# A Griffin-style decoder layer with a 32-expert mixture: the last two experts interleaved, and the attention scores' first part moved ahead of a weight split

## The chip, the cores and the metric

One core of one Trainium2 chip. The metric is the device time of one execution in microseconds (us), the median of three runs.

## The reference, cut to what matters

Batch 1, 256 tokens, width 1024, everything in fp32. First comes a mixing part, then a mixture of 32 experts, of which each token uses four, then a final RMSNorm:

```python
h = rmsnorm(x, norm_mix); proj = h @ w_in            # 1024 x 10256
# three branches: mLSTM (4 heads), forgetting attention (8 heads), memory attention (4 heads)
merged = sum_b sigmoid(gate_b) * (y_b @ w_branch[b]);  x = x + merged @ w_out
logits = t @ w_router + b_router;  top_v, top_i = top_k(logits, 4)     # t = rmsnorm(x, norm_moe)
combine = one_hot(top_i) weighted by softmax(top_v)
for each expert:                                     # w1 1024 x 2048, w2 1024 x 1024
    u = t @ w1 + b1
    g = minimum(u[:, :1024], 7);  lin = clip(u[:, 1024:], -7, 7)
    a = g * sigmoid(1.702 * g) * (lin + 1)
    out += combine[:, e] * (a @ w2 + b2)
return rmsnorm(x + out, norm_final)
```

## The kernel before, in words

Each engine runs its own instruction list; the order on each is the written order, and semaphores join them. There is no planner.

**Mixing part (about 0 to 422 us).** The projections are cut into 64 slots (`SLOTS`), two to each 2 MB unit of weights in a ring of three. ACT rounds a slot's weights (`round_weights`, L689), DVE subtracts to get the remainder (`split_weights`, L1024: 128x2048, called for slot i + 2 in slot i), and PE runs the three products of the parts (`project`). A table `STAGES` hangs other work behind the slots: for head h, `ml_scores` in slot 12+h, `fx_scores` in 24+h, `ca_scores` in 36+h, then turn and values one and two slots later. In each slot DVE does `drain(i)`, `split_weights(i + 2)` and then the stage's functions. A score function on DVE has a first part that ACT waits for (mask and row maximum, or bias and clamp, L1152, L1154, L1241 to L1244, L1250, L1251), a wait for ACT's exponential (for ml also for POOL's mask, L613), and a last part that PE waits for (L1161, or L1235 and L1237).

**Experts (about 422 us to the end).** Each expert's weights come as six 2 MB pieces, four of w1 (`W1`) and two of w2 (`W2`), into ten places used in turn; two spare places take the first two pieces of expert 25. SP issues piece n into a place when the piece ten earlier in it has been used (`place_used`). Up to 64 tokens of an expert are gathered. A product is `both_halves` (L1753, L1754): two matmuls with 64 stationary columns each, side by side on the array, for the low and high half of the output; one fp32 matmul is two instructions. PE's list for one expert is: layer one (four pieces), `gather` of the next tokens but one (same lines, from `sel`), `put` of the previous result into the four sum banks (L1871), turning the activations (L1836), biases (L1782, L1776), layer two's first piece, `turn_gathered` (L1766), its second piece, `turn_weighted` (L1812). DVE does the activation (L1361 to L1373), ACT the copies out of PSUM (L933 to L958). Experts 0 to 24 are in a loop, 25 to 31 are written out; after expert 25's layer one `add_tokens` (L1876) adds the residual to the sums.

**End.** `is_last` marks expert 31: its last w1 piece and last w2 piece come in halves (L468, L469, L472, L473), and its activations are turned in two parts. Then ACT copies the result (L958), PE does the last `put`, ACT squares the four 512-column sums (L981, `accum_out`) and takes the square root (L985), DVE multiplies by the inverse root and `norm_final` straight out of PSUM (L1439), and four DMAs write the output (L568, L570 on SP, L988 on ACT). `norm_final`, spread over 128 partitions (`gfin`, 512 KB), is loaded behind all weights (L543).

```python
def is_last(m, q):
    return isinstance(m, int) and m * TURN + q == NE - 1
for i in range(len(SLOTS)):            # DVE
    if i < len(SLOTS) - 1:
        drain(i)
    split_weights(i + 2)
    for name, *arg in STAGES.get(i, []):
        if name in work:
            work[name](*arg)
```

Of the kernel before, what the change touches and what calls it, by code (L numbers as in the profile page):

```python
# [4 lines left out]
F32 = mybir.dt.float32  # L5
# [6 lines left out]
P = 128  # L12
# [23 lines left out]
SPARE_PIECE = LOOPED * TURN * PIECES  # L36
CYCLE = TURN * PIECES // RING_PLACES
# [107 lines left out]
def build(nc, x, mem, norm_mix, w_in, b_ml_gates, conv_ml, ml_head_norm, b_fx_gate, norm_mem,  # L145
# [3 lines left out]
    with ctx:  # L149
# [6 lines left out]
        bank = [ctx.enter_context(nc.psum_tensor(f"bank{b}", [P, 512], F32)) for b in range(8)]  # L156
# [117 lines left out]
        with nc.sbuf_tensor("sq_dump", [P, TT, 2, 512], F32) as sq_dump:  # L274
# [23 lines left out]
        gfin = place[1][:, 0, :]  # L298
        results, final_dump = place[2][:, 0:TT, :], place[3][:, 0:TT, :]
# [11 lines left out]
        router_in, b1_in, b2_in, final_in, final_late_in, out_sent = (  # L311
            sem(n) for n in ("router_in", "b1_in", "b2_in", "final_in", "final_late_in", "out_sent"))
# [11 lines left out]
        ml_ready = sem("ml_ready")  # L324
        pre_zero = sem("pre_zero")
        conv_sum, conv_sig, qk_ready = sem("conv_sum"), sem("conv_sig"), sem("qk_ready")
        gate_lin, gate_log, gates_ready = sem("gate_lin"), sem("gate_log"), sem("gates_ready")
        act_step = sem("act_step")
        col_ready = sem("col_ready")
        ml_arg, ml_exp, ml_masked = sem("ml_arg"), sem("ml_exp"), sem("ml_masked")  # L330
        ml_num, ml_ms, ml_std, ml_y = sem("ml_num"), sem("ml_ms"), sem("ml_std"), sem("ml_y")
        max_ready, exp_ready, prob_ready, pt_ready, y_ready = (sem(n) for n in ("max_ready", "exp_ready", "prob_ready", "pt_ready", "y_ready"))
# [18 lines left out]
        final_ready = sem("final_ready")  # L351
        late_in = {j: sem(f"late_in{j}") for j in (W1 - 1, PIECES - 1)}
        late_actT, late_aT = sem("late_actT"), sem("late_aT")
# [56 lines left out]
        def is_last(m, q):  # L410

            return isinstance(m, int) and m * TURN + q == NE - 1

        def for_experts(eng, r, expert):

            with eng.Fori(0, LOOPED) as m:
                for q in range(TURN):
                    expert(r, m, q)
            for q in range(NE - LOOPED * TURN):
                expert(r, LOOPED + q // TURN, q % TURN)  # L420

# [25 lines left out]
        def _(sp):  # L447
# [5 lines left out]
            def load(e, j, b):  # L453

                halves = isinstance(e, int) and e == NE - 1 and j in late_in
# [9 lines left out]
                if halves and j < W1:  # L465

                    dst, src = (a.rearrange("p (q h n) -> p q h n", q=2, h=2) for a in (dst, src))
                    sp.dma_start(dst[:, :, 0], src[:, :, 0]).then_inc(late_in[j], 16)  # L468
                    sp.dma_start(dst[:, :, 1], src[:, :, 1]).then_inc(place_in[b], 16)  # L469
                elif halves:  # L470

                    sp.dma_start(dst[:, 0:2 * D], src[:, 0:2 * D]).then_inc(late_in[j], 16)  # L472
                    sp.dma_start(dst[:, 2 * D:4 * D], src[:, 2 * D:4 * D]).then_inc(place_in[b], 16)  # L473
                else:
                    sp.dma_start(dst, src).then_inc(place_in[b], 16)
# [65 lines left out]
            def load_final(loaded):  # L541

                sp.dma_start(gfin, norm_final.partition_broadcast(P)).then_inc(loaded, 16)  # L543
# [4 lines left out]
            for c in range(RING_PLACES, NE * PIECES - (LOOPED - 1) * TURN * PIECES):  # L548
                if not is_spare(LOOPED - 1, c):
                    load_piece(0, LOOPED - 1, c)  # L550
            sp.wait_ge(route_ready, 1)
            busiest = sp.value_load(most[0:1, 0:1], min_val=0, max_val=S)
            with sp.If(busiest < CAP + 1):
                sp.wait_ge(place_used[1], place_uses(1))
                load_final(final_in)
            with sp.If(busiest > CAP):
                with sp.Fori(1, ROUNDS) as r:
                    with sp.If(busiest > r * CAP):
                        with sp.Fori(0, LOOPED) as m:
                            for c in range(TURN * PIECES):  # L560
                                load_piece(r, m, c)
                        for c in range(NE * PIECES - SPARE_PIECE):
                            load_piece(r, LOOPED, c)
                sp.wait_ge(moe_end, 1)
                load_final(final_late_in)
# [3 lines left out]
            sp.wait_ge(final_ready, 4)  # L569
# [82 lines left out]
        def _(act):  # L652
# [277 lines left out]
            def expert(r, m, q):  # L930
                n = r * NE + m * TURN + q
                act.wait_ge(gate_ready, n + 1)
                act.activation(acts.rearrange("c (q p) -> c q p", q=4), gate, ACT.Sigmoid, scale=ALPHA).then_inc(sig_ready, 1)  # L933

                def keep_chosen():

                    act.wait_ge(selT_done, n + 1)
                    src = bank[LINEAR if is_last(m, q) else TURNS]
                    act.activation(selWT, src[:, 0:S].rearrange("p (t n) -> p t n", t=TT), ACT.Copy).then_inc(selWT_ready, 1)

                if is_last(m, q):
                    act.wait_ge(late_actT, r + 1)
                    act.activation(aT[:, 0:2], bank[TURNS][:, 0:2 * P].rearrange("p (q h c) -> p q h c", q=2, h=2),
                                   ACT.Copy).then_inc(late_aT, 1)
                    if isinstance(r, int):
                        warm(ACT.Sqrt)
                    act.wait_ge(act_turned, n + 1)
                    act.activation(aT[:, 2:4], bank[GATE][:, 0:2 * P].rearrange("p (q h c) -> p q h c", q=2, h=2),
                                   ACT.Copy).then_inc(aT_ready, 1)
                    keep_chosen()  # L950
                else:
                    keep_gathered(n + 2)
                    act.wait_ge(act_turned, n + 1)
                    act.activation(aT, bank[TURNS][:, :].rearrange("p (q h c) -> p q h c", q=4, h=2),
                                   ACT.Copy).then_inc(aT_ready, 1)
# [3 lines left out]
                if not is_last(m, q):  # L959
                    keep_chosen()  # L960
# [4 lines left out]
            def experts(r):  # L965
                for_experts(act, r, expert)

                act.wait_ge(got_ready, (r + 1) * NE)
                act.sem_inc(round_end, 1)

            def finish(rounds):

                if rounds:
                    warm(ACT.Sqrt)
                for t in range(TT):
                    for j in range(2):
                        if rounds:
                            act.wait_ge(moe_end, 1)
                        else:
                            act.wait_ge(put_done, 4 * NE + 2 * t + j + 1)  # L980
                        act.activation(final_dump[:, t, UW * j:UW * (j + 1)], bank[SUMS + 2 * t + j][:, :], ACT.Square,  # L981
                                       accum_out=ss[:, t, j:j + 1]).then_inc(final_sq, 1)
                    act.wait_ge(final_sq, 2 * t + 2)
                    act.wait_ge(final_var, t + 1)
                    act.activation(std[:, t, 0:1], ss[:, t, 1:2], ACT.Sqrt, bias=var[:, t:t + 1],  # L985
                                   scale=1.0 / D).then_inc(final_std, 1)
                act.wait_ge(final_ready, 3)
# [5 lines left out]
        def _(dve):  # L993
# [153 lines left out]
            def ml_scores(h):  # L1147
                dve.wait_ge(filled[5], turn(5, ("ml_m", h)))
                if h == 0:
# [5 lines left out]
                                  ALU.add, ALU.min).then_inc(drained[5], 1)  # L1155
                dve.wait_ge(ml_masked, 2 * h + 2)
# [82 lines left out]
            def fx_scores(h):  # L1239
# [4 lines left out]
                dve.tensor_reduce(negmax[:, 1:2], p_a[:, 128:384], AX.X, ALU.max, negate=True).then_inc(max_ready, 1)  # L1244
                dve.wait_ge(exp_ready, 2 * h + 2)
                normalise(((0, 128), (128, 384)))

            def ca_scores(h):
                dve.wait_ge(filled[4], turn(4, ("ca_s", h)))
                step(dve.tensor_reduce(negmax[:, :], bank[4][:, :].rearrange("p (t m) -> p t m", t=TT), AX.X, ALU.max))  # L1250
                dve.tensor_scalar(negmax[:, :], negmax[:, :], -CA_SCALE, None, ALU.mult).then_inc(max_ready, 1)  # L1251
                dve.wait_ge(exp_ready, 2 * FX_H + h + 1)
# [7 lines left out]
            for i in range(len(SLOTS)):  # L1260
# [3 lines left out]
                split_weights(i + 2)  # L1264
                for name, *arg in STAGES.get(i, []):
                    if name in work:
                        work[name](*arg)
# [79 lines left out]
            def take_turned(k):  # L1347
# [3 lines left out]
                for h in range(2):  # L1351
                    dve.tensor_tensor(gotT[:, :, h, :],  # L1352
                                      bank[TURNS][:, :].rearrange("p (q h c) -> p q h c", q=4, h=2)[:, :, h, :],
# [3 lines left out]
            def expert(r, m, q):  # L1357
                e = m * TURN + q
                n = r * NE + e
# [7 lines left out]
                blocks = acts.rearrange("c (q p) -> c q p", q=4)  # L1367
                dve.tensor_tensor(blocks, blocks, gate, ALU.mult).then_inc(ffn_step, 1)
                b, used = piece_turn(r, m, PIECES * q + W1 - 1)
# [6 lines left out]
                if not is_last(m, q):  # L1376
                    dve.wait_ge(gather_done, n + 2)
                    select(e + 2)
                    take_turned(n + 2)
                dve.wait_ge(selT_done, n + 1)  # L1380
                select_weighted(e + 1)

# [30 lines left out]
            def experts(r):  # L1413
                for_experts(dve, r, expert)
                dve.wait_ge(sel_ready, (r + 1) * (2 * (NE + 1)))
                dve.wait_ge(selW_ready, (r + 1) * (2 * (NE + 1)))
# [9 lines left out]
            def finish(rounds):  # L1426
# [3 lines left out]
                dve.wait_ge(final_late_in if rounds else final_in, 16)  # L1430
                for t in range(TT):
                    dve.wait_ge(final_sq, 2 * t + 1)
                    dve.tensor_scalar(var[:, t:t + 1], ss[:, t, 0:1], 1.0 / D, EPS, ALU.mult, ALU.add).then_inc(final_var, 1)
# [3 lines left out]
                    for j in range(2):  # L1437
# [479 lines left out]
```

## Time and profile before

| | us |
|---|---|
| median of three runs (lowest, highest) | 1327.95 (1327.43, 1328.49) |
| the profiled execution's own time | 1328.85 |
| its span, first to last instruction | 1326.9 |
| PE busy (share of the span) | 1291.2 (97%) |
| mean granted PE clock | 0.998 |

The profile is one execution. Times in its rows count from the start of its span. PE is the matmul engine and PEld its weight loads; a row of the time line is start, duration, engine, line, operation, output<-input, and in brackets how long the engine sat idle before it and who released it. Matmuls overlap, so the distance between two starts, and not the duration, is what one costs in a row.

### The profile page before, as it was taken

The numbers are of one execution on the slowest core, as the hardware profiler recorded it, in microseconds if no ns is written. First come the engines' busy times: TensorE is split into PE (matmuls) and PEld (weight loads), VectorE is DVE, ScalarE is ACT, GpSimd is POOL, SyncE is SP. The second block draws the span as 40 slices with busy tenths as digits, with TensorE's granted clock in tenths as the row PEclk, the third lists the DMA queues.
The fourth block names the chain that finished last, engine by engine and source line by source line (L and its number), as shares of the span: only waits on it lengthen the run. The fifth ranks groups of instructions, "written<-read, shape, count | busy, mean of one in ns | idle before, by whom it ended". The sixth has DMA issues, their size and how long they took to land.

```text
span 1326.9 us, 15133 instructions
## 1 busy us (share of the span) xinstructions
PE 1291.2 (97%) x6183; PEld 659.7 (50%) x6183; DVE 412.7 (31%) x736; ACT 323.4 (24%) x499; POOL 29.4 (2%) x42
## 2 busy tenths in 40 slices
PE   8999999999999999999999999999999999999997
PEld 8888888888887333333333333333333333333332
DVE  6864665545565121111211121111121111112112
ACT  5665555654444010100101010100011001001012
POOL 4000000000102000000000000000000000000000
PEclk9999999999999999999999999999999999999999
DMA  9553453536679999999999999999999999999996
GB/s 325 193 188 132 186 177 141 204 115 259 206 294 432 428 431 429 432 432 430 432 431 432 431 431 432 431 431 431 433 431 431 431 431 432 429 432 431 430 430 266
DMA packets 68030, 475.12 MB, mean 358 GB/s; under 512 B 7504, under 2 KB 9616, under 8 KB 43408
## 3 DMA queue, kind: packets, MB, share of 16 engines
q1 hardware_dynamic: 65840, 473.28, 85.9%
q10 hardware_dynamic: 2144, 1.21, 0.3%
q8 instruction: 31, 0.51, 0.1%
q14 instruction: 15, 0.12, 0.0%
HBM read 473.42 MB, written 1.05 MB: 358 GB/s over the span
## 4 chain that ended last, share of the span: by engine, by line
PE 75%; DMA 22%; DVE 1%; ACT 1%; issue 1%; SPq 0%; POOL 0%; DVEq 0%; ACTq 0%; POOLq 0%
PE bank L1753 37%; DMA place<-in_w_exp_in 22%; PE bank L1562 18%; PE bank L1541 4%; PE bank L1871 4%; PE bank L1542 2%; PE bank L1549 1%; PE bank L1836 1%; PE bank L1766 1%; PE bank L1776 1%; PE bank L1754 1%; DMA ring<-in_w_in 1%; PE bank L1685 1%; PE bank L1704 1%; PE bank L1812 1%
## 5 line engine op out<-in xcount | busy, mean ns | idle before, releaser
L1753 PE MATMUL bank<-place,fxqT 128*64 128x512 f32 x1520 | 677.5, 596 | 20.5 <-DMA place<-in_w_exp_in 19.5
L1754 PE MATMUL bank<-place,fxqT 128*64 128x512 f32 x1520 | 677.8, 596 | 0.0
L1753 PEld LDWEIGHTS bank<-place,fxqT 128*64 128x64 f32 x1520 | 198.3, 137 | 429.1 <-issue 389.1
L1754 PEld LDWEIGHTS bank<-place,fxqT 128*64 128x64 f32 x1520 | 198.3, 137 | 0.0
L1024 DVE TENSOR_TENSOR w_lo<-ring,w_hi 128x2048 fp32r<-128x2048 f32 x63 | 145.2, 2305 | 103.1 <-ACT w_hi L689 102.9
L689 ACT ACTIVATE w_hi<-ring 128x2048 fp32r<-128x2048 f32 x63 | 120.8, 1917 | 117.0 <-PE bank L1562 105.2
L1361 DVE TENSOR_SCALAR bank<-bank 128x512 f32<-128x512 f32 x32 | 22.4, 700 | 391.6 <-PE bank L1754 391.6
L1562 PE MATMUL bank<-w_hi,h_cat 128*128 128x512 f32 x448 | 141.1, 391 | 0.0
L933 ACT ACTIVATE fxqT<-bank 128x512 f32<-128x512 f32 x32 | 19.1, 598 | 414.1 <-DVE bank L1361 414.1
L1562 PEld LDWEIGHTS bank<-w_hi,h_cat 128*128 128x128 f32 x448 | 84.1, 188 | 17.4
L1352 DVE TENSOR_TENSOR fxqT<-bank,g_rows 128x256 f32<-128x256 f32 x64 | 24.2, 420 | 216.0 <-PE bank L1766 216.0
L1562 PE MATMUL bank<-w_lo,h_cat 128*128 128x512 f32 x224 | 87.2, 389 | 0.0
L1562 PE MATMUL bank<-w_hi,o_cat 128*128 128x512 f32 x256 | 82.0, 395 | 0.0
L958 ACT ACTIVATE yS<-bank 128x512 f32<-128x512 f32 x32 | 19.1, 598 | 249.3 <-PE bank L1754 249.3
L1541 PE MATMUL bank<-h_cat,w_hi 128*128 128x512 f32 x192 | 69.0, 402 | 0.0
L1871 PE MATMUL bank<-yS,fxqT 64*128 64x512 f32 x264 | 65.6, 615 | 0.8 <-ACT yS L958 0.8
L1753 PE MATMUL bank<-xs,sel 128*64 128x512 f32 x128 | 60.2, 592 | 0.2 <-DVE sel L1328 0.2
L1754 PE MATMUL bank<-xs,sel 128*64 128x512 f32 x128 | 60.2, 593 | 0.0
L1542 PE MATMUL bank<-h_cat,w_lo 128*128 128x256 f32 x192 | 53.9, 281 | 0.0
L1562 PEld LDWEIGHTS bank<-w_hi,o_cat 128*128 128x128 f32 x256 | 48.1, 188 | 10.2 <-DVE w_lo L1024 0.3
L1339 DVE TENSOR_SCALAR cols_wr<-slots_f,rank,comb 128x128 f32<-128x128 f32 x66 | 19.9, 344 | 106.8 <-PE bank L1812 106.8
L1562 PE MATMUL bank<-w_lo,o_cat 128*128 128x512 f32 x128 | 49.8, 389 | 0.0
(291 smaller groups left out, 1065.5 us busy)
## 6 DMA issues: line engine op xcount, KB each, us to landing
place<-in_w_exp_in SPq DMA_DIRECT2D x125, 2048.0 KB, 36.7
place<-in_w_exp_out SPq DMA_DIRECT2D x63, 2048.0 KB, 37.6
ring<-in_w_in SPq DMA_DIRECT2D x19, 2048.0 KB, 7.5
ring<-in_w_branch SPq DMA_DIRECT2D x6, 2048.0 KB, 7.7
ring<-in_w_mem_kv SPq DMA_DIRECT2D x4, 2048.0 KB, 7.7
ring<-in_w_out SPq DMA_DIRECT2D x2, 2048.0 KB, 11.1
spare<-in_w_exp_in SPq DMA_DIRECT2D x2, 2048.0 KB, 12.2
ring<-in_w_in SPq DMA_DIRECT2D x2, 1024.0 KB, 8.2
```

The costliest lines, as they stand in the source:

```text
L689: act.activation(hi, whole, ACT.Copy).then_inc(weights_rounded, 1)
L933: act.activation(acts.rearrange("c (q p) -> c q p", q=4), gate, ACT.Sigmoid, scale=ALPHA).then_inc(sig_ready, 1)
L1024: dve.tensor_tensor(lo, whole, hi.bitcast(F32), ALU.subtract).then_inc(weights_split, 1)
L1339: ins = dve.tensor_scalar(selW[:, t, :, :], twice, rank[:, t, bass.ds(e, 1)], comb[:, t, bass.ds(e, 1)], ALU.is_equal, ALU.mult)
L1352: dve.tensor_tensor(gotT[:, :, h, :], bank[TURNS][:, :].rearrange("p (q h c) -> p q h c", q=4, h=2)[:, :, h, :], weights[:, :, h].unsqueez ...
L1361: dve.tensor_scalar(bank[GATE][:, :], bank[GATE][:, :], LIMIT, None, ALU.min).then_inc(gate_ready, 1)
L1541: mm(slot_bank(i, c)[:, :], wh[:, k, tile], both, start=(k == 0), stop=False)
L1542: ins = mm(slot_bank(i, c)[:, 0:S], wl[:, k, tile], hi[:, k, :], start=False, stop=(k == KT - 1))
L1562: ins = mm(slot_bank(i, c)[:, :], stationary, moving, start=(k == 0 and n == 0), stop=(k == KT - 1 and n == 2))
L1753: mm(o[0:CAP, :], lhsT, low, start=start, stop=stop)
L1754: return mm(o[CAP:P, :], lhsT, high, start=start, stop=stop)
L1871: mm(bank[SUMS + q][:, :], selWT[half, t, :], yS[half, :], start=False, stop=last).then_inc(put_done, 1)
```

## The change: what it does

Two edits. **One**: the DVE functions `ml_scores`, `fx_scores` and `ca_scores` now call `split_weights(i + 2)` themselves, between their first part and their wait for ACT; in slots without scores it stays where it was. **Two**: `expert` runs experts 0 to 29 only, and `last_two` runs 30 and 31. Their pieces come, and are used, in the order w1 of 30, w1 of 31, w2 of 30, w2 of 31. The last w2 is loaded and computed by output halves: columns 0:512 of both pieces (1 MB each), then columns 512:1024 of the first piece (1 MB) and of the second in two row parts (512 KB each). So these are products of 256 columns a side, summed in the banks LINEAR and GATE; each half is copied and put into the sums on its own (`put_late`), and the squares of the first half's sums, and its product with `norm_final`, are made before the second half. `norm_final` comes as one 4 KB row behind a piece of expert 27 and is spread on PE with a column of ones in experts 27 and 28, DVE keeping the result (`GFIN_AT`); PE waits for that copy each time. At the end the unscaled results lie in SBUF and are scaled there, three quarters on DVE and one on ACT.

```diff
+LAST_ORDER = [(NE - 2 + n // W1, n % W1) for n in range(2 * W1)] + [(NE - 2 + n // W2, W1 + n % W2) for n in range(2 * W2)]
+GFIN_AT = (LOOPED * TURN + 2, LOOPED * TURN + 3)
+HALF = 256
@@ SP
+            def load_last_two(r):
+                for e, j in LAST_ORDER[:-W2]:
+                    b, used = late_turn(r, e, j)
+                    sp.wait_ge(place_used[b], used)
+                    load(e, j, b)
...
+                for j in range(W2):
+                    load_chunk(j, 0, slice(0, 4), place_in[late_turn(r, NE - 1, W1 + j)[0]])
+                load_chunk(0, 1, slice(0, 4), late_in[0])
+                for n in range(2):
+                    load_chunk(1, 1, slice(2 * n, 2 * n + 2), late_in[1 + n])
@@ DVE
-            def fx_scores(h):
+            def fx_scores(h, i):
...
                 dve.tensor_reduce(negmax[:, 1:2], p_a[:, 128:384], AX.X, ALU.max, negate=True).then_inc(max_ready, 1)
+                split_weights(i + 2)
                 dve.wait_ge(exp_ready, 2 * h + 2)
...
+                if isinstance(e, int) and e in GFIN_AT:
+                    h = GFIN_AT.index(e)
+                    dve.wait_ge(gfin_turned, r * 2 + (h + 1))
+                    dve.tensor_copy(gfin[:, 512 * h:512 * (h + 1)], bank[RESULT][:, :]).then_inc(gfin_kept, 1)
...
+            def keep_scaled(t, h, kept):
+                cut = slice(512 * h, 512 * (h + 1))
+                dve.tensor_tensor(results[:, t, cut], sums[:, t, h, :], gfin[:, cut], ALU.mult).then_inc(kept, 1)
@@ DVE, finish
+                    dve.wait_ge(put_done, 4 * NE + 4)
+                    keep_scaled(1, 1, final_kept)
+                    dve.wait_ge(final_sq, 1)
+                    keep_scaled(0, 1, final_kept)
...
-                    for j in range(2):
-                        dve.scalar_tensor_tensor(out=results[:, t, cut], in0=bank[SUMS + 2 * t + j][:, :], ...
+                    for j in range(t, 2):
+                        dve.tensor_scalar(results[:, t, cut], results[:, t, cut], rstd[:, t, 0:1], None, ALU.mult).then_inc(final_ready, 1)
@@ ACT, finish
+                    act.activation(dump, src, ACT.Square, accum_out=ss[:, t, 1:2]).then_inc(final_sq, 1)   # t = 1 waits for final_kept
...
+                act.activation(results[:, 1, 0:UW], results[:, 1, 0:UW], ACT.Copy, scale=rstd[:, 1, 0:1]).then_inc(final_scaled, 1)
@@ PE, in expert, between turn_acts and add_late_bias
+                if isinstance(e, int) and e in GFIN_AT:
...
+                    mm(bank[RESULT][:, :], ones_row, gfin_row[:, 512 * h:512 * (h + 1)], start=True, stop=True).then_inc(gfin_turned, 1)
+                    pe.wait_ge(gfin_kept, r * 2 + (h + 1))
@@ PE
+            def last_two(r):
+                layer_one(n, lambda j: late_turn(r, e, j))
...
+                gather(n * 2 + 4); put(n); turn_gathered(n + 2, RESULT)
+                turn_acts(acts, TURNS); add_biases(r, n + 1); add_late_bias(r, n)
+                layer_one(n + 1, lambda j: late_turn(r, e + 1, j))
+                layer_two(0, *late_turn(r, e, W1))
+                turn_weighted(r, n); turn_acts(acts_late, GATE); add_half_bias(LINEAR, 0)
+                turn_weighted(r, n + 1); add_half_bias(GATE, 1)
+                layer_two(1, *late_turn(r, e, W1 + 1))
...
+                chunk(bank[LINEAR], b0, 0, range(4), 0, False)
+                put(n + 1)
+                chunk(bank[LINEAR], b1, 1, range(4), 0, True).then_inc(chunk_done, 1)
+                chunk(bank[GATE], b0, 0, range(4), 1, False).then_inc(place_used[b0], 1)
+                put_late(r, 0)
+                for h in range(2):
+                    pe.wait_ge(late_in[1 + h], r * 16 + 16)
+                    ins = chunk(bank[GATE], b1, 1, range(2 * h, 2 * h + 2), 1, h == 1)
+                put_late(r, 1)
+            def put_late(r, h):
...
+                for swap in range(2):
+                    if swap:
+                        pe.wait_ge(done, before_ + 2)
+                    for t in range(TT):
+                        g = t ^ swap
+                        mm(sums[:, t, h, HALF * g:HALF * (g + 1)], selWT_late[rows_, t, :], yS_late[rows_, HALF * h:HALF * (h + 1)], ...
```

(Several calls with their waits between are written on one line here.)

## Rows read from the trace of the kernel before

**Rows 1.** Busy time by stretch: each engine's us (instructions), PEclk, DMA share, GB/s.
```profile
900.00:1000.00 100.00, 93.60 (x430) 32.07 (x428) 18.03 (x44) 11.08 (x19) 0.00 (x0) 1.00 1.01 431
```

**Rows 2.** All waits of PE between 20 and 420 us: us, times, longest.
```profile
PE bank L1668 <- DVE p_bt L1237: 1.6, 1, 1.6
PE bank L1645 <- DVE p_bt L1161: 1.0, 1, 1.0
```

**Rows 3.** Busy time by stretch, the same view as rows 1, for 1200 to 1300.
```profile
1200.00:1300.00 100.00, 98.25 (x454) 33.76 (x454) 15.83 (x40) 9.42 (x18) 0.00 (x0) 1.00 1.01 429
```

**Rows 4.** Time line of DVE, ACT and PE around the first forgetting head.
```profile
166.97 0.76 DVE L1056 TENSOR_TENSOR merged<-bank,merged 128x256 f32<-128x256 f32 x2 [2.11 <-ACT merged L705]
168.69 1.28 ACT L790 ACT_TABLE_LOAD   x1
168.71 2.29 DVE L1024 TENSOR_TENSOR w_lo<-ring,w_hi 128x2048 fp32r<-128x2048 f32 x1 [0.98 <-ACT w_hi L689]
...
173.29 0.17 DVE L1235 RECIPROCAL rsum<-esum 128x2 f32<-128x2 f32 x1 [1.05 <-ACT p_bt L792]
...
174.10 0.55 PE L1668 MATMUL bank<-ident,p_bt 128*128 128x128 f32 x3 [1.55 <-DVE p_bt L1237]
```

**Rows 5.** Time line of PE: w1 of expert 30, its gather and put, w1 of expert 31.
```profile
1274.35 0.64 PE L1753 MATMUL bank<-place,fxqT 128*64 128x512 f32 x1 [1.13 <-DMA place<-in_w_exp_in]
...
1277.84 0.59 PE L1753 MATMUL bank<-xs,sel 128*64 128x512 f32 x1
...
1279.65 1.99 PE L1871 MATMUL bank<-yS,fxqT 64*128 64x512 f32 x8
...
1298.74 0.61 PE L1753 MATMUL bank<-place,fxqT 128*64 128x512 f32 x1 [0.62 <-DMA place<-in_w_exp_in]
```

**Rows 6.** Time line of PE in expert 27, between its layers, and the put of expert 28.
```profile
1197.34 1.99 PE L1871 MATMUL bank<-yS,fxqT 64*128 64x512 f32 x8
1199.26 0.66 PE L1836 MATMUL bank<-ident,fxqT 128*128 128x128 f32 x4
1199.67 0.48 PE L1782 MATMUL bank<-b2split,pick_out 128*128 128x512 f32 x1
...
1224.33 1.99 PE L1871 MATMUL bank<-yS,fxqT 64*128 64x512 f32 x8
```

**Rows 7.** DMA to landing, last w2 piece's first half (L472), and second (L473); their issues.
```profile
DMA to landing us min/median/max: 34.8/34.8/34.8
...
DMA to landing us min/median/max: 29.7/29.7/29.7
...
1276.08 7.45 SPq L472 DMA_DIRECT2D place<-in_w_exp_out  x1
1283.58 4.21 SPq L473 DMA_DIRECT2D place<-in_w_exp_out  x1
```

**Rows 8.** Time line from the last products to the last issue.
```profile
1315.25 0.59 PE L1754 MATMUL bank<-place,fxqT 128*64 128x512 f32 x1
...
1315.68 0.59 PE L1754 MATMUL bank<-place,fxqT 128*64 128x512 f32 x1
1316.32 0.60 ACT L958 ACTIVATE yS<-bank 128x512 f32<-128x512 f32 x1 [3.21 <-PE bank L1754]
...
1317.06 1.99 PE L1871 MATMUL bank<-yS,fxqT 64*128 64x512 f32 x8 [0.79 <-ACT yS L958]
...
1318.19 0.60 ACT L981 ACTIVATE place<-bank 128x512 f32<-128x512 f32 x1 [1.27 <-PE bank L1871]
...
1323.54 0.33 SPq L570 DMA_DIRECT2D out_x<-place  x1
```

**Rows 9.** Groups of instructions by line and shape, DVE: total, mean ns.
```profile
L1361 DVE TENSOR_SCALAR bank<-bank 128x512 f32<-128x512 f32 x32 | 22.4, 700 | 391.6 <-PE bank L1754 391.6
...
L1237 DVE TENSOR_SCALAR p_bt<-p_bt,rsum 128x256 f32<-128x256 f32 x16 | 5.2, 349 | 0.1
```

**Rows 10.** Busy time by stretch, while only 2 KB packets of `w_in` and `w_mem_kv` move.
```profile
168.00:170.00 2.00, 2.00 (x14) 1.74 (x13) 1.29 (x1) 1.96 (x2) 0.00 (x0) 1.00 1.05 410
```

More of the change, by code:

```diff
@@ L408, in piece_turn, with late_turn, for_experts @@
             return b, r * place_uses(b) + used
[L410 to L414 removed]
+        def late_turn(r, e, j):
+            return piece_turn(r, LOOPED, LAST_TWO + LAST_ORDER.index((e, j)) - SPARE_PIECE)
+        def for_experts(eng, r, expert, last_two):
             with eng.Fori(0, LOOPED) as m:
@@ L418, in for_experts @@
                     expert(r, m, q)
-            for q in range(NE - LOOPED * TURN):
+            for q in range(NE - 2 - LOOPED * TURN):
                 expert(r, LOOPED + q // TURN, q % TURN)
+            last_two(r)
         def moe_turned(q, t):
@@ L464, in load @@
                 dst = place[b][:, :, :].rearrange("p k n -> p (k n)")
[L465 to L475, printed above, removed]
+                sp.dma_start(dst, src).then_inc(place_in[b], 16)
             def load_ahead(b):
@@ L931, in expert @@
                 n = r * NE + m * TURN + q
[L932 to L955, printed above, removed]
+                sigmoid(n, acts)
+                keep_gathered(n + 2)
+                keep_turned(n, TURNS, aT)
                 b, used = piece_turn(r, m, PIECES * q + PIECES - 1)
@@ L1263, in _ @@
                     drain(i)
-                split_weights(i + 2)
+                scores = {"ml_scores", "fx_scores", "ca_scores"}
+                if not any(name in scores for name, *arg in STAGES.get(i, [])):
+                    split_weights(i + 2)
                 for name, *arg in STAGES.get(i, []):
-                    if name in work:
+                    if name in scores:
+                        work[name](*arg, i)
+                    elif name in work:
                         work[name](*arg)
@@ L1865, in put, with turn_acts, turn_weighted @@
-            def put(k, last=False):
+            def turn_acts(src, b):
+                for g in range(4):
+                    ins = pe.transpose(bank[b][:, P * g:P * (g + 1)], src[:, P * g:P * (g + 1)], ident[:, :])
+                ins.then_inc(act_turned, 1)
+            def turn_weighted(r, n):
+                pe.wait_ge(selW_ready, n * 2 + 2)
+                for t in range(TT):
+                    ins = pe.transpose(bank[TURNS][:, P * t:P * (t + 1)],
+                                       selW[:, t, :, :].rearrange("p o c -> p (o c)"), ident[:, :])
+                ins.then_inc(selT_done, 1)
@@ new lines, in layer_two, with expert @@
+            def layer_two(j, b, used):
+                pe.wait_ge(place_in[b], used * 16 + 16)
+                for k in range(4):
+                    w = place[b][:, k, :]
+                    ins = both_halves(bank[RESULT], aT[:, k, j, :], w[:, 0:512], w[:, 512:D], False,
+                                      j == W2 - 1 and k == 3)
+                ins.then_inc(place_used[b], 1)
+            def expert(r, m, q):
+                e = m * TURN + q
+                n = r * NE + e
+                layer_one(n, lambda j: piece_turn(r, m, PIECES * q + j))
+                pe.wait_ge(selWT_ready, n + 1)
+                gather(n * 2 + 4)
+                put(n)
+                if isinstance(r, int) and isinstance(e, int) and e == LOOPED * TURN:
+                    add_tokens()
+                pe.wait_ge(act_ready, n + 1)
+                pe.wait_ge(got_ready, n + 2)
+                turn_acts(acts, TURNS)
+                if isinstance(e, int) and e in GFIN_AT:
+                    h = GFIN_AT.index(e)
+                    pe.wait_ge(ones_row_ready, r + 1)
+                    pe.wait_ge(gfin_in, r * 16 + 16)
+                    mm(bank[RESULT][:, :], ones_row, gfin_row[:, 512 * h:512 * (h + 1)], start=True, stop=True).then_inc(gfin_turned, 1)
+                    pe.wait_ge(gfin_kept, r * 2 + (h + 1))
+                add_late_bias(r, n)
+                add_biases(r, n + 1)
+                pe.wait_ge(aT_ready, n + 1)
+                layer_two(0, *piece_turn(r, m, PIECES * q + W1))
+                turn_gathered(n + 2)
+                layer_two(1, *piece_turn(r, m, PIECES * q + W1 + 1))
+                pe.wait_ge(gotT_ready, (n + 2) * 2)
+                turn_weighted(r, n)
@@ L1867, in put @@
+            def put(k):
                 pe.wait_ge(selWT_ready, k + 1)
@@ L1870, in put @@
                     t, half = q // 2, slice(CAP * (q % 2), CAP * (q % 2 + 1))
-                    mm(bank[SUMS + q][:, :], selWT[half, t, :], yS[half, :], start=False, stop=last).then_inc(put_done, 1)
+                    mm(bank[SUMS + q][:, :], selWT[half, t, :], yS[half, :], start=False, stop=False).then_inc(put_done, 1)
             def add_tokens():
@@ L1890, in experts @@
             def experts(r):
-                for_experts(pe, r, expert)
-                put((r + 1) * NE + r, last=True)
+                for_experts(pe, r, expert, last_two)
             for_rounds(pe, first_tokens, experts, read_late=True)
```

308 lines of the change are left out of this document (185 added, 123 removed).

## The prediction

> **What bounds the kernel now.** I read the page's 40 slices first, then the waits of PE, then the stretches, then the time line of the last 60 us.
>
> In the mixing part PE is the bound. Between 20 and 420 us it waited twice in all, 1.0 us for the first mLSTM head's weights of the scores and 1.6 us for the first forgetting head's [rows 2]. In the experts the weights are. The reader is to see DMA at 1.01 and 431 GB/s while PE is busy for 93.6 of 100 us [rows 1]: one expert is 12.58 MB, so 29.2 us of stream, and 27.0 us of PE (put to put) [rows 6]. Both start with the end of the mixing part, so a microsecond won there moves PE and stream alike.
>
> From expert 25 on this turns. Its first two pieces lie in the spare places since the mixing part, the stream is two pieces (9.7 us) ahead of PE, and PE works off that lead with 2.2 us an expert less 3.6 us for the residual. Only in experts 30 and 31 does it wait again, a start 1.3 us late at 1274.35 (the row shows 1.13, the matmul pipeline hides the rest) and 0.8 late at 1298.74 (0.62) [rows 5]. Between 1200 and 1300 PE was idle for 1.75 us, which are these two and nothing else [rows 3]. So what is added to its list in experts 27 and 28 arrives at its end, less what these waits swallow. The last weights land at 1283.6 + 29.7 = 1313.3 [rows 7], while the last product starts at 1315.7 [rows 8]. The end is PE's chain with the stream 3 us ahead of it, then 11 us of copy, put, squares, root, scaling, output.
>
> **The scores before the split.** Nothing is added; `split_weights` (2.29) changes places with a first part. Forgetting head 0: the drain that starts at 166.97 ends at 167.7. Mask and maxima then run to about 169.2, where before they came behind the split and ended at 172.2 (1.3 us). ACT has its table at 169.97 and is done with the exponential near 170.9. The split runs from 169.2 to 171.5, and the last part (0.81, from the reciprocal at 173.29 to PE's start at 174.10) lets PE start at 172.3 to 172.4 instead of 174.10 [rows 4]. Without the wait PE would have come at about 172.5: the 1.6 us go, with next to no margin, and I take 1.5. For mLSTM head 0 the clamp moves ahead of a split that starts when it did, since it waits for ACT's rounding; exponential and mask on POOL then lie beside the split, and the 1.0 us goes with about 1 us of margin. The later heads had no wait, so they win nothing. What is queued behind the moved split is the drain of the next slot and the ring's next load on SP. The split ends 0.5 to 1.2 us later than before in the forgetting slots, and PE needs it a slot later, with over 3 us to spare; a slot's ring load has a unit's time and more. Cost zero; if the cover fails, 16 slots pay up to 0.7 each. **Sum: -2.5** (bounds -2.65 and 0), on stream and PE together.
>
> **`norm_final` on PE.** Each half is one fp32 matmul of 512 columns, two instructions 0.43 apart, as are two starts in [rows 8]; then PE waits for DVE's copy. The nearest chain of this kind is the last result's: 0.64 from the last start to the copy's start, 0.14 from its end to the next matmul [rows 8]. DVE's PSUM instruction of 512 columns takes 0.70 [rows 9]. So 0.43 + 0.64 + 0.70 + 0.14 = 1.9, twice 3.8 us, in experts 27 and 28 where nothing hides them. Behind it stand the biases and layer two, for which ACT waits, then DVE's next selection; all of that moves with PE. Of the 3.8, the wait of 1.3 at expert 30 swallows as much: **PE comes 2.5 late to the gather of expert 30**, at 1280.3 instead of 1277.84 [rows 5]. The row itself is queued behind expert 27's fifth piece, and PE is some 7 us behind the stream there, so it will have landed. Bounds: 1.7 (matmuls alone, less the swallowed wait: 0.4) and 4.4 (DVE late by 0.3 each time: 3.1).
>
> **The last two experts on PE**, from that gather. Gather 1.8 (1277.84 to 1279.65), put 1.9, turning 0.4 [rows 5, 6], another turning and biases 1.4: layer one of expert 31 starts at 1286.0, four pieces at 3.42 end at 1299.7. Its pieces land from 1279 to 1294, one each 4.87 us from 1274.3 on, so it no longer waits; the 0.8 is gone, but as cover. Layer two's first piece of expert 30 landed at 1298.7: 1299.75 to 1303.2. Two turnings of the weighted selection, the turned activations and half biases with one short wait for ACT's copy: 2.1, estimated from 0.4 a turning. Second piece 1305.3 to 1308.75. Four chunks of 256 columns at half of 0.43 a start are 1.72 each, with the put 1.9: 1316.05. `put_late`, two pairs with a completion between, against 1.04 for two full instructions and their completion (1317.06 to 1318.1, just before ACT's square) [rows 8]: I take 1.1. The last chunk ends at 1318.95, where before the last product's stream ended at 1316.1: **+2.85**.
>
> Is the stream ever late? The last four MB come in 2 KB packets, at 410 GB/s as in the mixing part [rows 10] against 431: +0.5, so the last landing is 1313.8, and `norm_final`'s 512 KB behind it are gone. PE reaches that chunk at 1317.2. Hidden.
>
> *The Trainium skill, "DMA: Bandwidth & Descriptors", section Bandwidth, says to batch to 1 MiB or more, and that 1 MB alone takes 6.15 us. Here the last two MB landed at 1310.9 and 1313.3, 2.4 us apart [rows 7]: in a full queue the fixed part is hidden, and the trace speaks against using it so. By the rule the five chunks would take some 25 us and not 10.*
>
> **The end.** Before, from 1316.1 to the span's end 10.8. After: the last start of 256 columns plus 0.4, then ACT's half copy 0.4 (a half of 0.60, with its fixed part), 0.1 to PE, the second `put_late` 1.3 to its completion: 1321.0. The squares of one half a row are 0.7 each, with DVE's product (0.69, as a PSUM instruction) between them since the second waits for it: 1322.5. Two roots and a reciprocal, estimated at 0.3 each from ACT's fixed part: 1323.1. DVE's scaling from SBUF was not seen at 512 columns; it lies between 0.35 (256 columns) and 0.70 (512 from PSUM) [rows 9], I take 0.45, nearer to the first. There are three in a row, ACT's one beside them (0.60): the last issue at 1324.75 instead of 1323.54 [rows 8]. From there 3.36 as before: 1328.1. **So the second edit costs +1.2**: +2.85 on PE, -1.65 behind it. Bounds -2.0 (gfin 0.4, everything 0.5 tighter) and +3.5.
>
> **Sum.** -2.5 + 1.2 = -1.3 against the profiled execution (span 1326.9, own time 1328.85, of which 0.9 is its distance from the median of 1327.95). A difference carries over: 1327.95 - 1.3 = **1326.6**.
>
> **Rivals.**
> *The forecast*: both waits of the mixing part go, the second edit gives about one back. Chance 0.51. Its own range is 1325.2 to 1328.
>
> *The first edit wins little.* ACT's table load and rounding, not DVE's split, could set head 0's chain, or the wait could come back one slot on. For: the forgetting chain fits by 0.1 us only. Against: ACT idled 2.3 us before that exponential. With a gain of 0 to 1 the time is 1328.1 to 1329.2. Chance 0.15, all within the bound.
>
> *The end is the stream's, not PE's.* If the spread of `norm_final` costs PE no more than the 1.3 us that it waited anyway, and the small steps between the layers are hidden, the last chunk starts at its landing: 1313.8, plus 0.86, plus the tail of 9.1 = 1323.8 against 1326.9, and with the first edit -5.6: 1322.3; half way, 1324.5. For: the order was laid so that half a MB stands behind the last landing. Against: PE has no other idle time between 1200 and 1300 [rows 3]. Chance 0.22.
>
> *Slower: half width is not half time.* The four chunks, with 32 starts, give each weight load half the product to hide under. If the distance between starts stays at 0.43 they cost 32 x 0.21 = 6.8 more: 1333.4; at 0.28 (two loads of 0.14 in series) +2.1: 1328.8. It decides for slower from 0.34 up. Against: four turnings with 128 columns, each with a load twice as wide, start 0.1 apart (1199.26 to 1199.67) [rows 6]. Chance 0.08.
>
> *The change is not what it says to the stream*: the chunks, or the later ring loads, leave the queue dry near the end, or 2 KB packets run far below 410. Each us of it beyond 3.4 counts: 1328 to 1340. The rule above belongs here; by itself it would give about +12. Chance 0.04.
>
> **How the numbers follow.** About 0.2% (2.7 us) is what a measurement of this kernel tells from no change: faster is under 1325.3, slower over 1330.6. Faster: most of the stream rival (0.20) and the forecast's lower edge (0.09) = 0.29. Slower: half width above 0.34 (0.04) and the dry queue (0.03) = 0.07. Same 0.64. The range leaves out a tenth on each side: 1323.3, which takes in half of the stream rival, to 1329.2, the upper end of the first edit winning nothing.
>
> **What would show it.** PE's waits between 20 and 420 us gone and the first layer one 2.5 us earlier. In experts 27 and 28 a matmul from a row of ones, then a gap of some 1.5 us ended by DVE. No wait for weights from expert 30 on. 256-column starts 0.21 apart. Last chunk ending near 1316.5 of the new span, last weights landed near 1311.3, last issue near 1322.2. I am wrong if PE waits for weights among the last chunks, or if those starts lie 0.3 or more apart.

## The result and the profile after

The changed kernel takes **1331.57 us** (median of 18 runs, 1328.09 to 1332.43) against 1328.15 (18 runs) for the kernel before in the same runs: ratio 1.002, 95% interval 1.0012 to 1.0027, or +3.4 us. Forecast were 1326.6 and a range that ends at 1329.2. The profiled execution took 1330.1, its span 1328.1. In this and later comparisons a few executions of kernels that lack the change's one-row matmuls or PE's wait behind them, two of these 18 of the kernel before among them (1333.59 and 1333.94), took about 6 us longer, at a mean clock of 0.996 where it is listed; no trace of one was kept, and the medians do not rest on them.

The first edit did more than forecast. The waits of PE between 20 and 420 us are down from the two of [rows 2] to one of another kind:

```profile
PE bank L1854 <- DVE sel L1388: 0.2, 1, 0.2
```

In the time line of DVE, ACT and PE around the first forgetting head (in [rows 4] the split started at 168.71 and the reciprocal at 173.29) the mask and both maxima are ahead of the split, and the exponential runs beside it. The reciprocal needs the end of the split and comes 3.7 us earlier:

```profile
166.17 0.55 DVE L1295 TENSOR_TENSOR p_a<-sums,fxmask 128x384 f32<-128x384 f32 x1
...
167.22 1.28 ACT L816 ACT_TABLE_LOAD   x1
...
167.41 2.28 DVE L1077 TENSOR_TENSOR w_lo<-ring,w_hi 128x2048 fp32r<-128x2048 f32 x1
...
169.61 0.16 DVE L1289 RECIPROCAL rsum<-esum 128x2 f32<-128x2 f32 x1
```

The first expert's gather starts at 419.07 instead of 422.76 (-3.69, of which 0.24 is start-up).

The loss is in the experts. By stretch, 900 to 1300 answers to [rows 1, 3]; the short stretches show expert 28. The number behind POOL's is TensorE's granted clock: 0.73 and 0.85 are the lower level, 1.2 GHz, in parts of their stretch. The kernel before showed it only after its last matmul, from 1321 on.

```profile
900.00:1000.00 100.00, 94.75 (x436) 32.70 (x434) 18.55 (x46) 11.06 (x19) 0.00 (x0) 1.00 1.01 431
1222.00:1226.00 4.00, 3.71 (x16) 1.40 (x14) 0.48 (x2) 1.19 (x2) 0.00 (x0) 1.00 1.01 434
1226.00:1230.00 4.00, 3.51 (x11) 1.41 (x13) 0.88 (x3) 0.00 (x0) 0.00 (x0) 0.73 1.00 430
1230.00:1234.00 4.00, 4.00 (x18) 1.29 (x16) 0.64 (x2) 0.00 (x0) 0.00 (x0) 0.85 1.00 430
1200.00:1300.00 100.00, 99.19 (x451) 34.20 (x449) 18.28 (x43) 8.58 (x16) 0.00 (x0) 0.98 1.01 429
```

The time line of PE and DVE there, against [rows 6]: the pair from the row of ones (L1943), DVE's copy, PE's start behind it, then starts of 512 columns 0.86 apart instead of 0.43, four of them. The idle time that the view prints (0.78) counts from modelled ends.

```profile
1224.00 0.66 PE L1906 MATMUL bank<-ident,fxqT 128*128 128x128 f32 x4
...
1224.59 1.12 PE L1943 MATMUL bank<-spare 1*128 1x512 f32 x2
...
1225.74 0.69 DVE L1444 COPY spare<-bank 128x512 f32<-128x512 f32 x1 [3.52 <-PE bank L1943]
...
1226.49 0.50 PE L1883 MATMUL bank<-b2split,pick_out 128*128 128x512 f32 x1 [0.78 <-DVE spare L1444]
...
1228.74 1.06 PE L1854 MATMUL bank<-place,fxqT 128*64 128x512 f32 x1
...
1229.60 1.06 PE L1854 MATMUL bank<-place,fxqT 128*64 128x512 f32 x1
```

The puts of experts 27 to 30 start here:

```profile
1193.06 1.99 PE L2032 MATMUL sums<-yS,fxqT 64*128 64x512 f32 x8
...
1222.08 1.99 PE L2032 MATMUL sums<-yS,fxqT 64*128 64x512 f32 x8
...
1252.81 1.99 PE L2032 MATMUL sums<-yS,fxqT 64*128 64x512 f32 x8
...
1279.79 1.99 PE L2032 MATMUL sums<-yS,fxqT 64*128 64x512 f32 x8
```

The first distance is 29.02, where it was 26.99 [rows 6]: +2.03 for the pair and its wait. The second is +2.03 and +1.7 more, the four starts at half speed. This execution shows one such fall, in expert 28; in expert 27 the same pair and the same wait (0.78 printed) left the clock at 1.00. The median execution is 1.5 us longer at a lower mean clock (0.995 to 0.996 against 0.997).

The end, against [rows 8]: last products of 256 columns, ACT's half copy, the second `put_late` (L2023), squares and product, scalings, the last two issues.

```profile
1316.83 0.38 PE L1855 MATMUL bank<-place,spare 128*64 128x256 f32 x1
...
1317.04 0.38 PE L1855 MATMUL bank<-place,spare 128*64 128x256 f32 x1
1317.47 0.38 ACT L1005 ACTIVATE spare<-bank 128x256 f32<-128x256 f32 x1 [0.58 <-PE bank L1855]
...
1318.00 1.47 PE L2023 MATMUL sums<-spare 64*128 64x256 f32 x8 [0.58 <-ACT spare L1005]
...
1319.54 0.60 ACT L1031 ACTIVATE spare<-sums 128x512 f32<-128x512 f32 x1 [1.69 <-PE sums L2023]
...
1322.94 0.36 SPq L596 DMA_DIRECT2D out_x<-spare  x1
1323.17 0.38 ACTq L1041 DMA_DIRECT2D out_x<-spare  x1
```

And the output's DMA issues: count, KB each, median us from issue to landing. Before they were 2.9 (SP) and 2.5 (ACT).

```profile
out_x<-spare SPq DMA_DIRECT2D x3, 256.0 KB, 2.7
out_x<-spare ACTq DMA_DIRECT2D x1, 256.0 KB, 4.6
```

### The profile page after: what moved, and what is told of

Its sections match the earlier page's. It is cut to its first block, busy times and chain, and to the rows that moved or that the text cites. A ratio compares the mean times of both kernels' runs of the same rounds, so it can differ in the third digit from the quotient of the medians.

```text
span 1328.1 us, 15242 instructions
## 1 busy us (share of the span) xinstructions
PE 1295.9 (98%) x6234; PEld 664.8 (50%) x6234; DVE 412.9 (31%) x737; ACT 323.4 (24%) x500; POOL 32.3 (2%) x42
## 3 DMA queue, kind: packets, MB, share of 16 engines
HBM read 472.90 MB, written 1.05 MB: 357 GB/s over the span
## 4 chain that ended last, share of the span: by engine, by line
PE 82%; DMA 16%; DVE 1%; issue 0%; SPq 0%; ACT 0%; ACTq 0%; DVEq 0%
PE bank L1854 42%; PE bank L1663 18%; DMA place<-in_w_exp_in 16%; PE bank L1642 4%; PE sums L2032 4%; PE bank L1643 2%; PE bank L1650 1%; PE bank L1867 1%; PE bank L1906 1%; PE bank L1877 1%; PE bank L1855 1%; PE bank L1913 1%; PE bank L1883 1%; PE sums L1786 1%; PE sums L1805 1%; DMA ring<-in_w_in 1%
## 5 line engine op out<-in xcount | busy, mean ns | idle before, releaser
L2032 PE MATMUL sums<-yS,fxqT 64*128 64x512 f32 x256 | 63.6, 615 | 0.0
```

The source lines that it names most:

```text
L2032: mm(bank[SUMS + q][:, :], selWT[half, t, :], yS[half, :], start=False, stop=False).then_inc(put_done, 1)
```

## The experiments

Medians, with the number of runs; ratios are to the kernel before on the same chip (1327.97 to 1328.26 there). A difference between two kernels is one of their medians.

**1. The first edit alone.** The second edit is left off; the first is as in the change: `split_weights(i + 2)` inside the three `..._scores`, behind their first part.

> The kernel before with the first edit alone (the split of the weights behind the scores' first part). Both theories: the changed kernel reached its first expert 3.7 us earlier and its stream of weights ran 4.3 us earlier, so this one ends 4 us under the kernel before, near 1324. If most of the 3.7 us had come from elsewhere (start-up, the other edit) it ends within 1 us of the 2.65 that the two waits account for or above, 1325.5 to 1328.

Measured: **1324.52** (10 runs), ratio 0.9976 (0.9967 to 0.9986), -3.45 us. It beats both kernels. So the second edit costs 7.05 on top of it and not 1.2.

**2. PE's standstill filled.** Five small matmuls into an unused bank stand between the pair and PE's wait:

```diff
 mm(bank[RESULT][:, :], ones_row, gfin_row[...], ...).then_inc(gfin_turned, 1)
+keep_clock(GATE, 5, ident[:, :])
 pe.wait_ge(gfin_kept, ...)
```

> The changed kernel, with five 128-column matmuls into the free bank GATE in experts 27 and 28 while PE waits for DVE's copy of norm_final; the wait stays. Theory A (the clock falls to its lower level because PE stands still for about 0.95 us there): no stretch at the lower level before the end, the same place in time for layer two, so 1.7 us less than the changed kernel's profiled run and 3.4 us less than its usual one: about 1328. Theory B (the fall has nothing to do with the gap; or the time is the gap's alone): the lower level is still there, time as the changed kernel's, 1331 to 1332.

Measured: **1328.97** (11 runs), ratio 1.0008 (0.9999 to 1.0017), 2.6 less than the change, every run at 0.997 or 0.998. The time line of PE in expert 27 has the same pair and work in place of the gap. PE goes on 2.19 behind the pair's start, where the change has 1.90, but the clock stays at 2.4 GHz:

```profile
1195.18 1.12 PE L1943 MATMUL bank<-spare 1*128 1x512 f32 x2
...
1196.23 1.38 PE L1580 MATMUL bank<-ident 128*128 128x128 f32 x10
...
1197.37 0.48 PE L1883 MATMUL bank<-b2split,pick_out 128*128 128x512 f32 x1
```

**3. No wait on PE.** The pair goes to a bank that is read later, and the wait stands behind layer two's first piece:

```diff
-mm(bank[RESULT][:, :], ones_row, ...).then_inc(gfin_turned, 1)
-pe.wait_ge(gfin_kept, ...)
+mm(bank[GATE][:, :], ones_row, ...).then_inc(gfin_turned, 1)
 ...
 layer_two(0, ...)
+pe.wait_ge(gfin_kept, ...)
+add_biases(r, n + 1)
```

> The changed kernel, with norm_final spread into bank GATE and the biases of the next expert moved behind layer two's first piece in experts 27 and 28, so that PE has a piece of work while DVE copies. Theory A (gap and fall of the clock cost 2.3 + 3.4 us in the usual run): about 1331.6 - 3.4 - 2.3 = 1325.9, mean clock as the kernel before's. Theory B (the tail is what made it slower): no more than the 2.3 us of standing still goes, 1329.3.

Measured: **1327.09** (11 runs), ratio 0.9995 (0.9983 to 1.0008): 4.5 less than the change, and no lower level at the two places:

```profile
1190.00:1200.00 10.00, 10.00 (x46) 3.37 (x41) 3.72 (x9) 1.79 (x3) 0.00 (x0) 1.00 1.01 431
1220.00:1240.00 20.00, 20.00 (x91) 7.05 (x89) 3.78 (x9) 2.07 (x4) 0.00 (x0) 1.00 1.01 431
```

Here one-row matmuls without a standstill left the clock alone. The time lies between the two that were expected: the standstill was put at 2.3 us for both places and was worth less. From the put of expert 27 to that of 28 it is 28.23 us here and 28.84 with the wait at full clock (experiment 6), so 0.6 a place.

**4. and 5. The gap in the kernel before.** In experts 27 and 28 a pair of fp32 matmuls of 512 columns that nobody uses, and PE waits for DVE's copy, once with 128 rows of operands and once with one row, as the change has it:

```diff
 ins.then_inc(act_turned, 1)
+mm(bank[RESULT][:, :], ident[:, :], xs[:, 0, 0:512], ...).then_inc(gap_made, 1)        # 4
+mm(bank[RESULT][:, :], ident[0:1, :], xs[0:1, 0, 0:512], ...).then_inc(gap_made, 1)    # 5
+pe.wait_ge(gap_kept, ...)
```

> The kernel before with a matmul pair of 512 columns and a wait for DVE's copy of it in experts 27 and 28, at the place where the changed kernel has them (its copy goes to a spare place that nothing reads). Theory A: each costs 2.0 us of PE, of which the 2.1 us of waits for weights in experts 30 and 31 swallow half, and the clock falls after one or both: 2 + 1.7 to 3.4, so 1331.5 to 1333.5, mean clock 0.995 to 0.997. Theory B (the clock does not fall for such a gap): 1330, mean clock 0.998.

> As before_gap, but the matmul pair takes one row (1 partition) of its operands in place of 128, as the changed kernel's does; the gap behind it is the same. before_gap (128 rows) had no stretch at the lower clock and 1329.4. Theory A (the clock falls because the array had one row's work and then none, pair and gap together): the lower level shows after expert 27 or 28, 1.7 us each, 1331 to 1333, mean clock 0.995 to 0.997. Theory C (the rows don't matter; the changed kernel falls because of something else in its experts 25 to 29): 1329.4, mean clock 0.998.

Measured: 128 rows **1329.43** (11 runs), ratio 1.0012 (1.0003 to 1.0022); one row **1332.99** (7 runs), ratio 1.0032 (1.0021 to 1.0044). By stretch, first with 128 rows, then with one, around both gaps:

```profile
1200.00:1204.00 4.00, 3.39 (x15) 1.40 (x17) 1.00 (x3) 0.00 (x0) 0.00 (x0) 1.00 0.99 422
1228.00:1236.00 8.00, 7.21 (x33) 2.60 (x33) 1.89 (x5) 0.44 (x1) 0.00 (x0) 1.00 1.00 428
```

```profile
1200.00:1204.00 4.00, 3.77 (x9) 1.40 (x11) 0.62 (x3) 0.00 (x0) 0.00 (x0) 0.57 0.99 422
1228.00:1236.00 8.00, 7.22 (x26) 2.45 (x23) 1.14 (x3) 0.60 (x1) 0.00 (x0) 0.79 1.00 429
```

The gap itself is the same in both. In the time line of PE, first 128 rows, then one, the wait's row prints 0.79 and 0.78; behind it the two bias instructions take 0.62 with the one and 1.05 with the other.

```profile
1198.80 1.02 PE L1844 MATMUL bank<-xs,ident 128*128 128x512 f32 x2
...
1200.61 0.50 PE L1787 MATMUL bank<-b2split,pick_out 128*128 128x512 f32 x1 [0.79 <-DVE spare L1380]
...
1200.95 0.62 PE L1781 MATMUL bank<-b1split,pick_in 128*128 128x512 f32 x2
```

```profile
1198.33 1.12 PE L1844 MATMUL bank<-xs,ident 1*128 1x512 f32 x2
...
1200.23 0.53 PE L1787 MATMUL bank<-b2split,pick_out 128*128 128x512 f32 x1 [0.78 <-DVE spare L1380]
...
1200.57 1.05 PE L1781 MATMUL bank<-b1split,pick_in 128*128 128x512 f32 x2
```

So the first theory, that the standstill by itself lowers the clock, fell with number 4; number 5 costs 3.56 more than it by one difference only, the rows of the pair. From the put of expert 27 to that of 28 it is 26.99 without a gap, 28.84 with 128 rows and 30.64 with one. In the change, where the clock stayed up in expert 27 with one row, it was 29.02: about 0.2 a place is the one-row pair itself, the other 1.6 the lower clock.

**6. The change with all rows.** The row and the ones are 128 partitions deep, zeros below the first row; pair, wait and copy stay:

```diff
-gfin_row, ones_row = spares[1][0:1, 0, :], spares[1][0:1, 1, 0:P]
+gfin_row, ones_row = spares[1][:, 0, :], spares[1][:, 1, 0:P]
```

> The changed kernel with the pair taking 128 rows: the row's tile and the ones are 128 partitions, all rows but the first of the tile zero (DVE clears it in expert 25); the wait stays. Theory A: no lower level before the end, as with the gap filled: 1328.5 to 1329. Theory C: 1331.6, as the changed kernel.

Measured: **1328.01** (11 runs), ratio 0.9999 (0.999 to 1.0008): 3.56 less than the change. The stretch of expert 28's gap stays at 1.00:

```profile
1224.00:1232.00 8.00, 7.22 (x33) 2.85 (x34) 1.81 (x5) 0.60 (x1) 0.00 (x0) 1.00 1.01 434
```

**7. `norm_final` not on PE.** The 512 KB DMA of the kernel before is back, ahead of the last 2 MB of weights; pair, copies and waits are gone, the interleaved end stays:

```diff
+sp.dma_start(gfin, norm_final.partition_broadcast(P))
 load_chunk(0, 1, slice(0, 4), late_in[0])
```

> The changed kernel without norm_final on PE: it comes spread over 128 partitions by one 512 KB DMA ahead of the last w2's second output half; everything else stays. So it is the first edit and the interleaved end alone. If the interleaved order and its end are worth nothing by themselves (the same 11.1 us from the last product to the end of the span, and 1.6 us more of PE between expert 30's put and the last product than the order before), it ends at 1326, 1.5 above the first edit alone. If they are worth what they are made for (the stream's last landing near 1309.6 plus 0.9 and the tail), 1322 to 1323.

Measured: **1326.96** (11 runs), ratio 0.9996 (0.9987 to 1.0005). Against experiment 1 this is the interleaved end by itself: **+2.44**. Against experiment 6 the pair and its wait at full clock: 1.05. The waits of PE from 1200 on (us, times, longest), here and then in experiment 1:

```profile
PE bank L1845 <- DMA place<-in_w_exp_out: 1.2, 1, 1.2
PE bank L1845 <- DMA place<-in_w_exp_in: 1.1, 1, 1.1
```

```profile
PE bank L1760 <- DMA place<-in_w_exp_in: 1.7, 2, 1.1
...
PE bank L1878 <- ACT yS L958: 0.8, 1, 0.8
```

Without the gaps PE catches up with the stream, and a wait for w2 of expert 30 is new. That is why pair and gaps, 3.7 long in experiment 6 (28.84 between puts for 26.99, twice), cost only 1.05: for most of it PE would have waited for weights. There is no wait for the last chunks, so the 512 KB ahead of them cost nothing.

**8. The second edit alone.** The scores' first part is behind the split again, as before.

> The changed kernel without the first edit. If the two edits add up, 1331.6 + 3.5 = 1335.0, 7 over the kernel before. If the first edit's lead is what lets PE run into its gaps at the wrong time (the fall of the clock tied to where PE stands against the stream), the lower level is gone and it ends near 1332.

Measured: **1333.83** (5 runs), ratio 1.0042 (1.0028 to 1.0055), with falls of the clock at both gaps. It is 2.26 above the change, where the first edit won 3.45 by itself. So the edits neither add up to the 1335.0 of the first expectation nor is the lower level gone, as the second would have it.

**9. to 11. The slow last DMA.** In the interleaved end the last 256 KB take 4.6 us to land. Three kernels ask whether the DMAs beside it or its queue do this: experiment 7 and experiment 1, each without the two output DMAs of tokens 0 to 127, and experiment 7 with the last DMA issued by SP instead of ACT.

```diff
-for n, cut in enumerate((slice(0, UW), slice(UW, D))):          # 9 and 10
-    sp.wait_ge(final_ready, n + 1)
-    sp.dma_start(out[0, 0:P, cut], results[:, 0, cut]).then_inc(out_sent, 16)
```

```diff
-act.dma_start(out[0, P:S, 0:UW], results[:, 1, 0:UW])...        # 11
+sp.wait_ge(final_scaled, 1)
+sp.dma_start(out[0, P:S, 0:UW], results[:, 1, 0:UW])...
```

> dma_late without the two output DMAs of tokens 0 to 127 (that half of the output is left unwritten); everything up to them is unchanged. Its four output DMAs are issued within 1.2 us and ACT's, the last, takes 4.6 us to land. Theory D (they queue behind one another on the same 16 engines, 1.05 MB at about 400 GB/s): the last lands 1.3 to 2 us earlier, 1325.0 to 1325.7. Theory E (the 4.6 us are ACT's queue, or the write itself): less than 0.4 us goes, 1326.6 or more.

> scores_only without the same two output DMAs. There these were issued 2.1 to 2.8 us ahead of the last one, which took 2.9 us to land. Theory D: they had moved by then, so nothing or at most 0.3 us goes: 1324.2 to 1324.5. Theory E: the same as for dma_late_half.

> dma_late with its last output DMA (tokens 128 to 255, columns 0 to 511) issued by SP instead of ACT; nothing else differs. In dma_late ACT's DMA took 4.7 us to land, SP's issued 0.24 us before it 2.9. Theory F (the DMA issued from ACT's queue at that moment is slow, whatever else moves): it lands 2.9 us after SP's issue at 1320.45, 1.5 us earlier: 1325.4. Theory G (the last DMA is slow on whichever queue, by its data's place or the write): 1327.

Measured: **1326.89** (11 runs), where experiment 7 has 1326.96, and **1324.51** (12 runs), where experiment 1 has 1324.52; with SP **1327.10** (11 runs). Half of the output costs nothing at either end, and neither the neighbours nor the queue are the cause: that DMA took 4.1 us alone with one other, and 4.2 from SP. The view of one line of the last kernel, its last issue (shortest, median, longest):

```profile
DMA to landing us min/median/max: 4.2/4.2/4.2
```

Why it lands late stays open. Two differences between the two ends were not tried apart: the memory that it reads (a spare place instead of a place), and that it follows the scaling by ACT. Against the first speaks that the three other DMAs of the interleaved end read the same spare place and landed in 2.1 to 2.9 us, the one issued 0.23 us ahead of it in 2.9.

## Why the prediction was wrong

**The bound.** Right. PE had no wait for weights from expert 29 on, and its end set the time; the stream's end was hidden, so that rival did not come in the change.

**The first edit, -2.5.** Right mechanism, too small a size. Both waits went; -3.45 was measured alone. Beside the two waits (1.2 and 1.77 at the two heads) 0.24 is start-up and 0.4 come from the other forgetting heads and the first memory head, to which the text gave nothing. On top of the second edit it was worth 2.26; why not 3.45 there was not settled.

**`norm_final`, "1.9, twice 3.8 us, in experts 27 and 28 where nothing hides them".** The size was right (2.03 each) and so was the swallowing: the put of expert 30 starts at 1279.79 against 1279.65 [rows 5], where +2.5 - 2.5 said no change. But it came out right for two errors that met: -4.28 at the put of expert 27 instead of -2.5, and 1.7 us of lower clock. **This is the step that failed.** It counted the standstill as its own length and took 0.43 a start for what stands behind it, where the trace has 0.86 at the lower level; no rival had the clock. Four combinations show what it takes: one row and a standstill, the clock falls (the change, experiments 5 and 8); 128 rows and a standstill, it doesn't (4 and 6); one row, filled (2) or without a wait (3), it doesn't. It takes both, and the one row in place of 128 costs 3.56, once in the change (1331.57 - 1328.01), once in the kernel before (1332.99 - 1329.43); some 0.4 of it is the pair itself, the rest the clock. Both together are not always enough: in the profiled execution expert 27's left the clock up, and one of the 18 executions of the change took 1328.09. What decides it then is not shown.

**The last two experts on PE, +0.35 beyond the late start.** Measured from the put of expert 30: 37.46 to the end of the last chunk (last start at 1317.04 and 0.21), where before it was 36.45, so +1.0, which is 0.65 more than forecast. Layer one of expert 31 began 3.92 behind that put, as worked out (3.9), and half width was half time (starts 0.213 apart), which ends the rival of the slow loads. What was too small are the small steps: `put_late` took 1.42 from its first start to the next product (1314.05 to 1315.47), not 1.1, the turnings and half biases between the layers 2.3, not 2.1, and changes from one kind of product to the next about 0.1 each, which the text left out.

**The end, -1.65.** Measured: 1317.25 to 1328.1, 10.85 against 10.8, so nothing was won, and this term was 1.7 too good. Copy, put, squares, roots and scalings came out: last issue 5.92 behind the last chunk, forecast 5.80. "From there 3.36 as before" was wrong: 4.93, since that DMA took 4.6 to land. The chain to the last issue is 1.5 shorter, and its last link gave 1.6 back; why it took so long was not found (experiments 9 to 11).

**The sum.** From the first edit alone to the change, by medians: 2.44 for the interleaved end, 1.05 for pair and wait, 3.56 for the one row and the clock. They are differences of neighbours in one chain of kernels, so that they give the 7.05 proves nothing by itself. Without the last term the forecast would have been 1.4 too low and in its range: experiment 6 has 1328.01. That 1.4 is the 1.7 of the end and the 0.65 on PE, less the 0.95 that the first edit won beyond its forecast.

## What to carry to other kernels

A small matmul put between others is paid not by its length alone: ask whether PE then stands still, and if it does, look at the granted clock behind it; the same product with all 128 rows, or with its wait moved behind other work, was 3.6 to 4.5 us better here. Where two edits come together, time each alone: here the first was worth 3.45 us and the pair cost 3.4, and the best version is experiment 1. A chain shortened ahead of a last DMA is won only when that DMA has been seen to land as fast as before.

## What was not expected of the hardware

- The granted clock fell behind a pair of fp32 matmuls of one row and 512 columns with a standstill of about 1 us (0.78 printed), and not behind the same with 128 rows: mean granted clock 0.57 and 1.00 in the same 4 us. *The Trainium skill, "TensorE: Matmul & The Clock Gate", section What's actually happening, says that the gate follows how busy PE has been. Here two kernels with the same list on PE and the same standstill differ in the rows of one pair alone, and one falls; of rows that section says nothing.*
- Stationary tiles of 64 columns with 256 moving ones in fp32 keep their pace: starts 0.213 apart, half of the 0.43 for 512 [rows 8].
- The last 256 KB output DMA took 4.1 to 4.7 us to land in every kernel with the interleaved end, from either queue; in the kernels without it no median of the output's issues was above 3.4. The cause stays open.
